# Gated delta rule in a one-core hybrid kernel: heads in two pairs, the next chunk's first products beside the state update

## The reference, cut to what matters

```
A    = where(strict, einsum(kb, kc) * L, 0)          # kb = beta * k, L = exp(G_i - G_j)
rhs  = concat([v * beta, kb * exp(G)])
u, w = triangular_solve(A + I, rhs)                  # per chunk and head
attn = einsum(q, k) * L
def step(state, ...):
    v_new = u_n - w_n @ state
    o     = qd_n @ state + attn_n @ v_new
    state = state * cd_n + kd_n^T @ v_new
```

## Time and profile before

| | |
|---|---|
| median of 3 runs | 3864.75 us (3854.51, 3864.75, 3866.74) |
| profiled execution, first to last instruction | 3856.7 us |
| median less that span (launch and end, and the spread of the runs) | 8.05 us |
| PE busy | 3463.8 us, 90% |
| PE weight loads busy | 2777.9 us, 72% |
| DVE / POOL / ACT busy | 1803.7 / 1581.2 / 908.5 us |
| mean granted TensorE clock | 0.951 |
| eight chunks, first product to last | 303.2 to about 848.6 us of the span |

### The profile page before, as it was taken

The page is one execution under the profiler, slowest core; times in us unless marked ns, Lnnn a source line. Parts: engine busy times, 40 slices in busy tenths (PEclk is TensorE's granted clock), DMA queues, the critical chain, the costliest instruction groups (busy, mean ns, idle before and its releaser), DMA issues.

```text
span 3856.7 us, 43293 instructions
## 1 busy us (share of the span) xinstructions
PE 3463.8 (90%) x16228; PEld 2777.9 (72%) x16228; DVE 1803.7 (47%) x2368; ACT 908.5 (24%) x1689; POOL 1581.2 (41%) x2013
## 2 busy tenths in 40 slices
PE   7998899978978999979899898889868989999988
PEld 6777888867865667757677577777756767678867
DVE  5763323236794454653523546474543344222333
ACT  3232212122002342323112322222221122210021
POOL 3544832204692224533354254243313434334523
PEclk9999999979999999989999999899979999999999
DMA  3122321102222012121112110000002101111211
GB/s 112 50 71 66 104 66 55 55 6 77 53 84 76 20 31 66 39 93 41 46 47 88 69 44 28 23 28 28 28 12 79 55 23 48 46 54 37 82 36 66
DMA packets 300658, 205.30 MB, mean 53 GB/s; under 512 B 25749, under 2 KB 277657, under 8 KB 300473
## 3 DMA queue, kind: packets, MB, share of 16 engines
q1 hardware_dynamic: 271241, 132.77, 12.5%
q10 hardware_dynamic: 29232, 69.95, 5.0%
HBM read 173.06 MB, written 29.63 MB: 53 GB/s over the span
## 4 chain that ended last, share of the span: by engine, by line
PE 61%; DVE 15%; ACT 4%; POOL 4%; issue 2%; PEld 1%; ACTq 1%; DMA 1%; PEldq 1%; DVEq 0%; POOLq 0%; SPq 0%
PE ps L343 45%; PE ps L1417 4%; PE ps L889 3%; DVE wrk L753 3%; POOL w_lo L2676 2%; ACT wrk L917 2%; PE ps L902 1%; POOL w_hi L2671 1%; PE ps L1788 1%; DVE wrk L942 1%; PE ps L2159 1%; DVE small L945 1%; PE ps L779 1%; DVE wrk L732 1%; PEld ps L2185 1%
## 5 line engine op out<-in xcount | busy, mean ns | idle before, releaser
L2671 POOL TENSOR_TENSOR w_hi<-w_raw,pool_one 128x256 fp32r<-128x256 f32 x1004 | 688.9, 715 | 2223.1 <-PE ps L343 2190.8
L343 PE MATMUL ps<-h_hi,w_hi 128*128 128x512 f32 x2928 | 1207.1, 412 | 83.2 <-POOL w_lo L2676 23.8
L343 PE MATMUL ps<-h_lo,w_hi 128*128 128x512 f32 x2928 | 1154.3, 394 | 0.0
L343 PE MATMUL ps<-h_hi,w_lo 128*128 128x512 f32 x2928 | 1154.0, 394 | 0.0
L2676 POOL TENSOR_TENSOR w_lo<-w_raw,w_hi 128x256 fp32r<-128x256 f32 x1004 | 893.4, 918 | 23.2
L343 PEld LDWEIGHTS ps<-h_hi,w_hi 128*128 128x128 f32 x2928 | 558.4, 191 | 258.7 <-issue 100.8
L343 PEld LDWEIGHTS ps<-h_hi,w_lo 128*128 128x128 f32 x2928 | 557.5, 190 | 121.4
L343 PEld LDWEIGHTS ps<-h_lo,w_hi 128*128 128x128 f32 x2928 | 559.9, 191 | 113.7 <-issue 9.4
L343 PE MATMUL ps<-y_hi,w_hi 128*128 128x512 f32 x704 | 290.8, 413 | 30.9 <-issue 30.1
L343 PE MATMUL ps<-y_hi,w_lo 128*128 128x512 f32 x704 | 277.5, 394 | 0.0
L343 PE MATMUL ps<-y_lo,w_hi 128*128 128x512 f32 x704 | 277.3, 394 | 0.0
(11 more groups left out here) (358 smaller groups left out, 3798.6 us busy)
## 6 DMA issues: line engine op xcount, KB each, us to landing
w_raw<-in_w_in SPq DMA_DIRECT2D x87, 512.0 KB
w_raw<-in_even_w_in SPq DMA_DIRECT2D x48, 512.0 KB
away<-wrk ACTq DMA_DIRECT2D x80, 256.0 KB, 2.0
wrk<-away ACTq DMA_DIRECT2D x32, 512.0 KB
w_raw<-in_odd_w_in SPq DMA_DIRECT2D x32, 512.0 KB
wrk<-in_x ACTq DMA_DIRECT2D x16, 512.0 KB, 8.1
w_raw<-in_w_br SPq DMA_DIRECT2D x32, 256.0 KB
w_raw<-in_even_w_out SPq DMA_DIRECT2D x24, 256.0 KB
```

Source lines behind the costliest of these rows:

```text
L343: mm = nc.tensor.matmul(ps[:, b, 0:n], w[:, slot, k, :], rhs(part, k, b), start=(k == 0 and q == 0), stop=(k == nk - 1 and q == 2))
L2671: ins = nc.gpsimd.tensor_tensor(hi, raw, one[:, 0:2], ALU.mult)
```

## The change

- **Pairs.** In the doubling steps and behind them, heads 0 and 1 and heads 2 and 3 go as two pairs. Every step of PE, ScalarE and VectorE is done once for each pair, on half the columns (256 for 512), with a semaphore count for each. Pair 0 uses banks 2, 4, 6 and pair 1 banks 3, 5, 7 (`p1` in 2 + p, `p3` in 4 + p, `p4` in 6 + p). The masks stay whole.
- **First products.** The spread decays and betas, the transposes of v and k k^T move into a function of their own, which is issued on PE in the state stage of the chunk in front (and ahead of chunk 0). k q^T and the transposes of k stay in the chunk. On ScalarE `exp` of the spread decays goes behind that of the decay matrix; on VectorE the scaling of q and `ATT` go behind the first steps.
- **Due times.** `CHUNK_TIME` goes from 70 to 52 and the state stage from 2 to 4 planned us; the points within a chunk are counted in 52nds. This alone decides how many dense pieces stand beside a chunk.

```diff
@@ -43,7 +43,7 @@
 
 REL_BUCKETS, REL_MAX_DIST, WINDOW = 32, 128, 128
 NLEVEL = 7
-CHUNK_TIME = 70.0
+CHUNK_TIME = 52.0
...
+    PE_STEPS = ["spread", "kk", "kq", "turned"]
+    ACT_STEPS = ["eg", "decays", "scaled"]
+    DVE_STEPS = ["decay logs", "nbeg", "mask 0", "u 0", "t 0", "mask 1", "att"]
+    for lv in range(1, L):
+        PE_STEPS += [f"p1 {lv} {p}" for p in range(2)]
+        ACT_STEPS += [f"z {lv} {p}" for p in range(2)]
+        if lv < L - 1:
+            DVE_STEPS.append(f"mask {lv + 1}")
+        for p in range(2):
...
+    lev_at = lambda lv: (9 + 6 * (lv - 1)) / 52
+
+    def products(dst, lhsT, rhs, heads=range(4)):
+        for h in heads:
+            mm = nc.tensor.matmul(four(dst)[:, h, :], lhsT(h), rhs(h), start=True, stop=True)
+        return mm
+
+    def first_products(pe, n):
+        c = slice(n * P, (n + 1) * P)
+        products(4, lambda h: gc_t[:, n, 4 + h:5 + h].to_broadcast([P, P]), lambda h: ident)
+        products(5, lambda h: beta_t[:, n, h:h + 1].to_broadcast([P, P]), lambda h: ident).then_inc(gdn_pe.sem, 1)
+        for h in range(4):
+            nc.tensor.transpose(four(3)[:, h, :], wt(h)[:, c], ident)
+        products(7, lambda h: acc[:, 4 + h, c], lambda h: acc[:, 4 + h, c]).then_inc(gdn_pe.sem, 1)
...
+            products(6, lambda h: acc[:, 4 + h, c], lambda h: acc[:, h, c]).then_inc(gdn_pe.sem, 1)
+            yield 5 / 52
+            pe.wait_ge(*step_dve("mask 0"))
             for h in range(4):
-                mm = nc.tensor.transpose(four(2)[:, h, :], BT[:, h, :], ident)
+                mm = nc.tensor.transpose(four(5)[:, h, :], BT[:, h, :], ident)
             mm.then_inc(gdn_pe.sem, 1)
             for lv in range(1, L):
                 yield lev_at(lv)
-                pe.wait_ge(*step_dve(3 + 2 * lv))
-                products(2, lambda h: BT[:, h, :], lambda h: TT[:, h, :]).then_inc(gdn_pe.sem, 1)
-                yield lev_at(lv) + 2 / 40
-                pe.wait_ge(*step_act(2 + lv))
-                if lv < L - 1:
-                    products(3, lambda h: UU[:, h, :], lambda h: ZZ[:, h, :])
-                products(4, lambda h: ZZ[:, h, :], lambda h: UU[:, h, :]).then_inc(gdn_pe.sem, 1)
-            yield 33 / 40
-            pe.wait_ge(*step_dve(2 + 2 * L))
-            products(6, lambda h: KBE[:, h, :], lambda h: UU[:, h, :]).then_inc(gdn_pe.sem, 1)
-            yield 35 / 40
-            pe.wait_ge(*step_act(2 + L))
-            for h in range(4):
-                mm = nc.tensor.matmul(four(5)[:, h, :], UU[:, h, :], VB[:, h, :], start=True, stop=(n == 0))
-                if n > 0:
-                    mm = nc.tensor.matmul(four(5)[:, h, :], ZZ[:, h, :], ST[:, h, :], start=False, stop=True)
-            mm.then_inc(gdn_pe.sem, 1)
-            yield 37 / 40
-            pe.wait_ge(*step_dve(3 + 2 * L))
-            for h in range(4):
-                if n > 0:
-                    nc.tensor.matmul(four(7)[:, h, :], ST[:, h, :], acc[:, h, c], start=True, stop=False)
-                nc.tensor.matmul(four(7)[:, h, :], TT[:, h, :], ATT[:, h, :], start=(n == 0), stop=True)
-            products(2, lambda h: KDEC[:, h, :], lambda h: TT[:, h, :])
+                pe.wait_ge(*step_dve(f"mask {lv}"))
+                if lv == 1:
+                    pe.wait_ge(*step_act("scaled"))
+                    pe.wait_ge(*step_dve("t 0"))
+                for p, _, heads in pairs:
+                    if lv > 1:
+                        pe.wait_ge(*step_dve(f"t {lv - 1} {p}"))
+                    products(2 + p, lambda h: BT[:, h, :], lambda h: TT[:, h, :], heads).then_inc(gdn_pe.sem, 1)
+                yield lev_at(lv) + 2.5 / 52
+                for p, _, heads in pairs:
+                    pe.wait_ge(*step_act(f"z {lv} {p}"))
+                    pe.wait_ge(*step_dve(f"u {lv - 1} {p}" if lv > 1 else "u 0"))
+                    if lv == 1 and p == 0:
+                        pe.wait_ge(*step_dve("att"))
+                    if lv < L - 1:
+                        products(4 + p, lambda h: UU[:, h, :], lambda h: ZZ[:, h, :], heads).then_inc(gdn_pe.sem, 1)
+                    products(6 + p, lambda h: ZZ[:, h, :], lambda h: UU[:, h, :], heads).then_inc(gdn_pe.sem, 1)
...
+            yield 50 / 52
+            for p, _, heads in pairs:
+                pe.wait_ge(*step_dve(f"v {p}"))
+                for h in heads:
+                    if n > 0:
+                        nc.tensor.matmul(four(6)[:, h, :], ST[:, h, :], acc[:, h, c], start=True, stop=False)
+                    nc.tensor.matmul(four(6)[:, h, :], TT[:, h, :], ATT[:, h, :], start=(n == 0), stop=True)
+                products(2, lambda h: KDEC[:, h, :], lambda h: TT[:, h, :], heads)
...
+            for lv in range(1, L + 1):
+                yield (lev_at(lv) if lv < L else 45 / 52) + 1 / 52
+                for p, two, _ in pairs:
+                    act.wait_ge(*step_pe(f"p1 {lv} {p}" if lv < L else f"p6 {p}"))
+                    nc.scalar.activation(ZZ[:, two, :], four(2 + p)[:, two, :],
+                                         ACT.Copy).then_inc(gdn_act.sem, 1)
...
+                yield lev_at(lv) + 3.5 / 52
+                for p, two, _ in pairs:
+                    if lv < L - 1:
+                        dve.wait_ge(*step_pe(f"p3 {lv} {p}"))
+                        nc.vector.tensor_tensor(TT[:, two, :], TT[:, two, :], four(4 + p)[:, two, :],
+                                                ALU.subtract).then_inc(gdn_dve.sem, 1)
+                    dve.wait_ge(*step_pe(f"p4 {lv} {p}"))
+                    nc.vector.tensor_tensor(UU[:, two, :], UU[:, two, :], four(6 + p)[:, two, :],
+                                            ALU.subtract).then_inc(gdn_dve.sem, 1)
...
+        if n == 0:
+            stage("A chunk 0 first products", 4.0, pe=lambda pe: first_products(pe, 0))
         stage(f"A chunk {n}", CHUNK_TIME, pe=f_pe, act=f_act, dve=f_dve)
...
-            nc.scalar.activation(acc[:, 0:4, c], four(7), ACT.Copy)
+            nc.scalar.activation(acc[:, 0:4, c], four(6), ACT.Copy)
...
-        stage(f"A chunk {n} state", 2.0, act=s_act, dve=s_dve)
+        more = {"pe": lambda pe: first_products(pe, n + 1)} if n < 7 else {}
+        stage(f"A chunk {n} state", 4.0, act=s_act, dve=s_dve, **more)
```

More of the change, by code:

```diff
@@ new lines, in _hybrid @@
+    PE_STEPS += ["p6 0", "p6 1", "p5 0", "p5 1"]
+    ACT_STEPS += [f"z {L} 0", f"z {L} 1"]
+    DVE_STEPS += ["v 0", "v 1"]
+    gdn_pe = sig.take("gdn_pe", 8 * len(PE_STEPS))
+    gdn_act = sig.take("gdn_act", 8 * len(ACT_STEPS))
+    gdn_dve = sig.take("gdn_dve", 8 * len(DVE_STEPS))
+    lev_at = lambda lv: (9 + 6 * (lv - 1)) / 52
[3 more added lines that the diff above has]
+        return mm
@@ L1414, in f_pe @@
+        pairs = [(p, slice(2 * p, 2 * p + 2), range(2 * p, 2 * p + 2)) for p in range(2)]
         def f_pe(pe):
-            def products(dst, lhsT, rhs):
-                for h in range(4):
-                    mm = nc.tensor.matmul(four(dst)[:, h, :], lhsT(h), rhs(h), start=True, stop=True)
-                return mm
             for h in range(4):
                 nc.tensor.transpose(four(2)[:, h, :], acc[:, 4 + h, c], ident)
-                nc.tensor.transpose(four(3)[:, h, :], wt(h)[:, c], ident)
@@ new lines, in f_pe @@
+            yield 45 / 52
+            for p, _, heads in pairs:
+                pe.wait_ge(*step_dve(f"u {L - 1} {p}"))
+                products(2 + p, lambda h: KBE[:, h, :], lambda h: UU[:, h, :], heads).then_inc(gdn_pe.sem, 1)
+            yield 47 / 52
+            for p, _, heads in pairs:
+                pe.wait_ge(*step_act(f"z {L} {p}"))
+                for h in heads:
+                    mm = nc.tensor.matmul(four(4 + p)[:, h, :], UU[:, h, :], VB[:, h, :], start=True, stop=(n == 0))
+                    if n > 0:
+                        mm = nc.tensor.matmul(four(4 + p)[:, h, :], ZZ[:, h, :], ST[:, h, :], start=False, stop=True)
+                mm.then_inc(gdn_pe.sem, 1)
@@ L1470, in f_act @@
-            act.wait_ge(*step_dve(1))
+            nc.scalar.activation(EG, four(4), ACT.Exp)
+            yield 2.5 / 52
+            act.wait_ge(*step_pe("kq"))
+            act.wait_ge(*step_act("decays"))
+            act.wait_ge(*step_dve("nbeg"))
             for h in range(4):
@@ L1503, in f_dve @@
[L1503 to L1506 removed]
+            dve.wait_ge(*step_dve("mask 0"))
+            nc.vector.tensor_tensor(UU, all4(ident), BT, ALU.subtract).then_inc(gdn_dve.sem, 1)
+            yield 6.5 / 52
+            dve.wait_ge(*step_pe("turned"))
+            nc.vector.tensor_tensor(TT, all4(ident), four(5), ALU.subtract).then_inc(gdn_dve.sem, 1)
@@ L1521, in delta_chunk @@
+            yield 48.5 / 52
+            for p, two, _ in pairs:
+                dve.wait_ge(*step_pe(f"p5 {p}"))
+                nc.vector.tensor_copy(TT[:, two, :], four(4 + p)[:, two, :]).then_inc(gdn_dve.sem, 1)
+        if n == 0:
+            stage("A chunk 0 first products", 4.0, pe=lambda pe: first_products(pe, 0))
```

(2 more changed lines are left out.)

80 lines of the change are left out of this document (27 added, 53 removed).

## The result

The changed kernel takes 3804.57 us (median of 4 runs, 3803.41 to 3806.69) against 3859.63 us (4 runs of the kernel before beside it); the ratio is 0.9851, with a 95% interval of 0.9833 to 0.9868. That is 55 us less. The forecast was 3795 us, 70 less; the time lies in the stated range.

The account below looks back on a forecast made before the run. PE was taken to bound the kernel, with 99.3 us lost to waits and half clock; 29.5 left (narrow tiles 10, chunks 16.5, turn 3) gives a 69.8 us gain, 3795 us, range 3776 to 3828.

Parts of the forecast that it names:

- PE bounds, and the 99 us of waits and half clock are all that can be won: Eight-chunk stretch: 446.1 us of PE work stays; only 99.3 of its 545.4 us can be gained.
- Chunk 7 covered, tail of 96 matmuls and 22 us: Chunk 7 gets dense matmuls around every step, most of its 41.8 us loss goes; 96 matmuls, 22 us, remain behind.
- I price the steps at nothing: Doubling steps: pairs' operands are ready before PE asks, despite less dense cover, so no loss; at worst 34 us.
- Lost after: 5.5 chunks 3.0 each: Chunks outside the narrow tiles each still lose 3.0 us, as chunk 5 did: 16.5 us in all.
- GpSimd is so close that I take 10: Narrow tiles: PE's work rises to about 133 us against GpSimd's 125, so the 23.0 us lost falls to 10.
- The turn, "+2.6, say 3": Section's end: last copy and store in view make PE wait about 4.7 us, not 2.08; 3 us lost, bounds 0 to 5.
- The first transpose's chain: First products to first transpose: chain of some 4.5 us, covered by 6.8 or 5.7 us; waits of 18.2 and 6.3 go.
- GpSimd rival: Narrow tiles: GpSimd's split and PE's tile take turns, all 23 us remain; gain 57, 3808 us; chance 0.17.
- The thin cover: Steps: leaner dense cover doesn't hold, half of 34 us is paid plus the 23; gain 40, 3825 us; chance 0.12.
- The falling clock: Short waits at the pairs' products spread chunk 7's 0.67 clock to other chunks; over half the stretch, 3905 us; chance 0.03.
- The median stands 8.05 above that span, which I keep: Whole kernel: 8.05 us between profiled span and median is kept, so a 3786.9 us span gives 3795 us.
- the step's account: Chunk 7's step: twelve records of 0.111 us at full clock would take 2.66 us, against 7.92 from start to start.

Follow-up runs that it names:

- 4: Changed kernel with all four heads together again (one group of 512 columns), new due times and moved first products kept: 3804.65 us.
- 11: Both 9 and 10 together: heads whole, old waits in the steps, first products in their own chunk, new due times kept: 3806.1 us.
- 10: As 4, but the first products are issued at the head of their own chunk, behind the state stage: 3801.5 us.
- 9: As 4, but with the old step waits: `p1` waits for both subtractions and the first subtraction for `p4`: 3814.0 us.
- 3: Changed kernel, with ScalarE's store wait in the memories' key and value stages moved to the first copy overwriting the buffer: 3796.0 us.
- 5: Changed kernel with heads whole and the old due times (CHUNK_TIME 70, state stage 2): 3831.7 us.
- 2: Changed kernel, pairs kept, with the old due times (CHUNK_TIME 70, state stage 2): 3818.0 us.
- 7: As 3, but the section's closing wait for the last stores moves to the first Silu that uses the buffer: 3792.2 us.

## Why the prediction was right, and where it was off

- **PE bounds, and the 99 us of waits and half clock are all that can be won:** right. The work stayed at 3146 records in the stretch, and the loss fell from 100.1 to 41.6 us (stretch less 446.1 us of work).
- **Chunk 7 covered, tail of 96 matmuls and 22 us:** right, to 0.1 us.
- **"I price the steps at nothing":** right for the changed kernel. But the term gave the pairs the credit. 4 shows that whole heads do as well in the total, with three short waits more; the finer waits that came with them are worth 5 to 10 us (11 against 10, 9 against 4).
- **"Lost after: 5.5 chunks 3.0 each":** too much. Chunk 6's period lost 0.7 us, and all that was lost outside the narrow tiles and the turn is 41.6 - 28.8 - 3.9 = 8.9 us, not 16.5. With the steps' and the transpose's waits gone, little of that kind was left.
- **"GpSimd is so close that I take 10" for the narrow tiles:** this is the term that was mis-sized, 28.8 us lost for 10, and I had named only one of the engines. 3 shows 8 us of it to come from ScalarE's wait for the stores' landing, half as idle time and half as the lower clock behind it, which I had left out altogether. The earlier trace rows show such a wait, 3.01 us; I priced it once, at the turn, and not at the six narrow stages that begin with it. GpSimd's low parts are the larger wait once it is gone (9.0 us), and the remaining 12 us or so no run takes apart. That the copies behind it became urgent because less dense work stands beside a chunk is my reading; no run shows it by itself. The work in these tiles was 140 us, too, not 133: the window of 140.5 us from which I scaled it up leaves out the first of them.
- **The turn, "+2.6, say 3":** PE's wait was 3.9 us against 2.08. Its second part, 2.9 us at the lower clock behind it, I had left out.
- **The first transpose's chain:** its waits went, as forecast, and the chain from VectorE's start to the mask, priced at some 4.5 us, takes 4.2 (11). But I gave the gain to the early first products. 10 and 11 show that these gain nothing, and that VectorE's earlier start in the shorter chain does.
- **The rivals.** The GpSimd rival's time, 3808, is near the measured one, and its mechanism only partly there: PE waited 3.4 us for it. The thin cover didn't come. The falling clock didn't come over the stretch, where it rose from 0.94 to 0.98, but it did in the narrow tiles (0.98 to 0.96) and at the turn.
- **"The median stands 8.05 above that span, which I keep":** this term was wrong, and it helped. Every run's time is 1.7 to 2.7 us above its own span; the rest of the 8.05 was that the profiled execution of the kernel before (3856.7 us of span) was quicker than the median one. In the changed kernel the profiled one is 3806.7 us, the median 3804.6, so it stands 0.2 us *below* the profiled span. The span was forecast at 3786.9 us and is 3804.8, 17.9 off; the median is 9.6 off. Some 8 us of the closeness are luck.
- **A slip in the step's account:** "twelve records" of full-clock work should be 24 (twelve products); the 2.66 us worked out from them are right.

The sum closes so, on the spans. The stretch: 100.1 us lost before, less 41.6 lost after (28.8 in the narrow tiles for 10, 8.9 in the other chunks for 16.5, 3.9 at the turn for 3), is 58.5. From that go 2.9 us of low clock behind the turn, 1.8 of the later start and 2.0 that stay open: 51.8, against 51.9 measured and 69.8 forecast.

## What to carry to other kernels

When a serial chain is woven into dense work, first spread the dense work over the whole chain, and then shorten what the dense pieces don't cover; a finer split of the chain pays where it runs alone (8.9 us here) and hardly under cover (2 us). Undo each part of such a change by itself: here the two in its title, the pairs and the early first products, were worth nothing that the total time shows. In the stretch the due times alone took 19.7 us, the earlier and shorter work between the first products and the first mask (with what the clock gave back) 36.3 more, and the finer waits 5.6 more; the move of the first products and the pairs then changed it by 2.8 and 0.3 us the wrong way. When a wait is named after the last of several releasers, look up when the others ended before you credit the one that is named. In an in-order queue put the wait for a store's landing at the first instruction that overwrites its buffer.

## What the runs showed of the hardware

- A lonely chunk of the same 228 records took 67.2 us at a granted clock of 0.67 (before), 45.1 us at 0.92 (5) and 36.2 us at 0.95 (2). In all three the clock was 1.00 over the first products and fell to its lower level behind PE's waits for the first transpose and the first step (6.3 and 1.5 us before, 2.5 and 1.4 in 5, 2.6 and 1.4 in 2). In 5 it was 0.50 from 786 to 790 us and 1.00 again from 794, with one wait of 0.7 us in each step; in the kernel before it was 0.50 from 790 to 814 and 0.62 to 0.77 behind that, with two waits in each step, 0.69 and 1.38 us. Whether the waits in the steps or the longer one ahead of them kept it down isn't shown: no run changed one without the other.
- PE's wait of 3.9 us at the turn was followed by 6.2 us of work at the lower level that is 3.3 us at the upper one. In 3 the same wait was followed by only some 3 us at that level, and with waits of 2.1 to 2.2 us there (before, 7) the clock stayed at 1.00.
- ScalarE waited 2.3 us for one store of 256 KB at the turn, and 3.0 to 7.0 us for two of them in the narrow stages. While it waited the 7.0 us, DMA moved 152 GB/s; at the turn 69.
